# Cross attention's scores and outputs from operands split in rounded half and rest, in a two-block transformer kernel

## The reference

```python
def memory_cross_attention(h, m, wq, wk, wv, wo):      # h = rms_norm(x), m = rms_norm(mem)
    q = (h @ wq).reshape(B, S, CROSS_HEADS, CROSS_DH)  # 256 tokens, 4 heads of 256
    k = (m @ wk).reshape(B, M, CROSS_HEADS, CROSS_DH)
    v = (m @ wv).reshape(B, M, CROSS_HEADS, CROSS_DH)
    s = jnp.einsum('bshd,bmhd->bhsm', q, k).astype(jnp.float32) * (CROSS_DH ** -0.5)
    p = jax.nn.softmax(s, axis=-1).astype(h.dtype)
    o = jnp.einsum('bhsm,bmhd->bshd', p, v).reshape(B, S, D_MODEL)
    return o @ wo
```

## Time and profile before

| what | value |
| --- | --- |
| median of 3 runs | 2339.91 us (2339.79 to 2341.52) |
| the profiled execution | 2339.71 us, its span 2337.9 us |
| TensorE busy | 2327.7 us, 100% |
| VectorE busy | 1549.7 us, 66% |
| ScalarE busy | 1203.0 us, 51% |
| granted TensorE clock over the span | 0.999 |

### The profile page before, as it was taken

How to read it: one execution, slowest core, us unless ns; L and a number is a source line. 1 busy time by engine, 2 the same in 40 slices (tenths; PEclk the granted TensorE clock), 3 DMA queues, 4 the chain that set the end, 5 groups by cost and what they waited for, 6 DMA issues and landing times.

```text
span 2337.9 us, 33592 instructions
## 1 busy us (share of the span) xinstructions
PE 2327.7 (100%) x13127; PEld 2008.6 (86%) x13127; DVE 1549.7 (66%) x1427; ACT 1203.0 (51%) x1209; POOL 79.7 (3%) x47
## 2 busy tenths in 40 slices
PE   9999999999999999999999999999999999999999
PEld 8889888888888898888888888888888888888887
DVE  6667866666666687556667666476667667467666
ACT  5447665544544575545445445664445444565444
POOL 0000510000000033000000000000000000000000
PEclk9999999999999999999999999999999999999999
DMA  9555444555565563536556656546655556555653
GB/s 308 187 194 177 149 155 162 171 187 190 189 195 186 185 188 129 168 122 224 187 183 223 193 188 194 162 153 207 192 190 187 194 188 198 181 163 165 204 187 118
DMA packets 328903, 427.95 MB, mean 183 GB/s; under 512 B 15528, under 2 KB 294320, under 8 KB 328560
## 3 DMA queue, kind: packets, MB, share of 16 engines
q1 hardware_dynamic: 324832, 412.73, 55.0%
q10 hardware_dynamic: 3984, 13.97, 1.6%
HBM read 425.60 MB, written 1.05 MB: 182 GB/s over the span
## 4 chain that ended last, share of the span: by engine, by line
PE 96%; DVE 2%; ACT 1%; issue 1%; ACTq 0%; DVEq 0%
PE ps L1122 25%; PE ps L1008 17%; PE ps L1009 17%; PE ps L1010 17%; PE ps L1126 13%; PE ps L1021 1%; DVE wlo L1673 1%; PE ps L1482 1%; PE ps L1460 1%; ACT whi L511 1%; PE ps L1316 0%; DVE arena L2011 0%; PE ps L1384 0%; PE ps L1394 0%; PE ps L1532 0%
## 5 line engine op out<-in xcount | busy, mean ns | idle before, releaser
L1673 DVE TENSOR_TENSOR wlo<-raw,whi 128x2048 fp32r<-128x2048 f32 x390 | 897.8, 2303 | 513.1 <-ACT whi L511 512.9
L511 ACT ACTIVATE whi<-raw 128x2048 fp32r<-128x2048 f32 x392 | 746.3, 1905 | 559.0 <-PE ps L1010 330.7
L1122 PE MATMUL ps<-hT,whi 128*128 128x512 f32 x2560 | 610.7, 390 | 0.0
L1122 PEld LDWEIGHTS ps<-hT,whi 128*128 128x128 f32 x2560 | 474.9, 188 | 95.1
L1008 PE MATMUL ps<-whi,hT 128*128 128x512 f32 x920 | 369.1, 401 | 0.2
L1010 PE MATMUL ps<-whi,hT 128*128 128x512 f32 x920 | 359.3, 391 | 0.0
L1009 PE MATMUL ps<-wlo,hT 128*128 128x512 f32 x920 | 358.8, 390 | 0.0
L1126 PEld LDWEIGHTS ps<-hT,wlo 128*128 128x128 f32 x2560 | 329.3, 191 | 13.1
L1126 PE MATMUL ps<-hT,wlo 128*128 128x256 f32 x2560 | 333.3, 283 | 0.0
L1008 PE MATMUL ps<-whi,aT_hi 128*128 128x512 f32 x640 | 250.0, 391 | 0.0
L1009 PE MATMUL ps<-wlo,aT_hi 128*128 128x512 f32 x640 | 250.0, 391 | 0.0
(11 more groups left out here) (296 smaller groups left out, 1949.5 us busy)
## 6 DMA issues: line engine op xcount, KB each, us to landing
raw<-in_w_ffn SPq DMA_DIRECT2D x264, 512.0 KB, 4.3
raw<-in_w_in SPq DMA_DIRECT2D x144, 512.0 KB, 4.8
raw<-in_ffn_w_down SPq DMA_DIRECT2D x88, 512.0 KB, 4.2
raw<-in_ffn_w_up SPq DMA_DIRECT2D x86, 512.0 KB, 4.0
raw<-in_ffn_w_gate SPq DMA_DIRECT2D x86, 512.0 KB, 4.9
raw<-in_w_out SPq DMA_DIRECT2D x32, 512.0 KB, 4.1
gain<-in_gains ACTq DMA_DIRECT2D x16, 512.0 KB
raw<-in_cross_wk SPq DMA_DIRECT2D x16, 512.0 KB, 4.2
```

Of the source, the lines that this page charges most:

```text
L511: act.activation(whi[:, s, :, 0:cols], raw[:, s, :, 0:cols], ACT.Copy).then_inc(hi_ready, 1)
L1122: pe.matmul(ps[:, G + n, :], whi[:, s, k, n * P:(n + 1) * P], both[k], start=first and k == 0, stop=False, skip_group_check=True)
L1673: dve.tensor_tensor(wlo[:, s, :, 0:cols], raw[:, s, :, 0:cols], whi[:, s, :, 0:cols].bitcast(F32), ALU.subtract).then_inc(lo_ready, 1)
```

## The change

Every product of cross attention's scores and outputs becomes three products of rounded half and rest, and both parts are made for all four of its operands. The new tiles lie at the same addresses as the float32 ones of the arena, under the type float32r (`rounded`).

- `banks_out` writes the rounded half of keys and values and signals `kv_hi`; the new `rest_out(n)` on DVE waits for it, subtracts the half from the two PSUM banks, and signals that the banks are free. `TAKEN` now names V for these.
- `query_out(i)` on ACT copies the two banks of the unscaled queries as rounded half, `queries(i)` on DVE is now the subtraction. The inverse root and the 1/16 become a column of two numbers (`sst[:, 3, 8:10]`), which `cross_exp` takes as a per-partition scale beside its per-partition bias, and by which `cross_max` multiplies the maximum. `row` and `row_out` are gone here.
- `prob_lo(h)` on DVE subtracts the rounded probabilities from PSUM; `cross_turn(h + 1)` and `cross_out(h)` wait for it (`c_pT_lo`) instead of `cross_pT`.

```diff
-TAKEN = ("SVVVVSS" "SSSSVV", "SVSSSSSSSSS")
+TAKEN = ("SVVVVSS" "VVVVVV", "SVSSSSSSSSS")
...
             def banks_out(b, l, u, banks, dst):
...
-                last.then_inc(chunk_out, 1)
+                last.then_inc(kv_hi, 1)
...
-                row_out(row_no(0, l, 2))
+                def query_out(i):
+                    wait_unit(act, 0, l, A_Q + 2 * i + 1)
+                    for n, bank in enumerate(Q_BANKS[i]):
+                        act.activation(query_hi[i][:, n * 512:(n + 1) * 512], ps[:, bank, :], ACT.Copy).then_inc(c_query, 1)
+                query_out(0)
...
-                                              bias=sst[:, 1, i:i + 1], accum_out=sst[:, 2, i:i + 1])
+                                              scale=sst[:, 3, 8 + t:9 + t], bias=sst[:, 1, i:i + 1], accum_out=sst[:, 2, i:i + 1])
...
-                            mm = pe.matmul(ps[:, TR + h % 2, t * SEQ:(t + 1) * SEQ], q[:, at + t * P:at + (t + 1) * P], k_[:, at:at + SEQ],
-                                           start=(k == 0), stop=(k == 1))
+                            mm = split_product(ps[:, TR + h % 2, t * SEQ:(t + 1) * SEQ], query_hi[i][:, q], query_lo[i][:, q],
+                                               key_hi[i][:, keys], key_lo[i][:, keys], k == t == 0, k == 1)
...
-                            mm = pe.matmul(ps[:, HEAD_BANKS[h], j * SEQ:(j + 1) * SEQ], v[:, at:at + P], cp_t[h % 2][:, k * SEQ:(k + 1) * SEQ],
-                                           start=(k == 0), stop=(k == 1))
+                            mm = split_product(ps[:, HEAD_BANKS[h], j * SEQ:(j + 1) * SEQ], value_hi[i][:, v], value_lo[i][:, v],
+                                               cp_hi[h % 2][:, keys], cp_lo[h % 2][:, keys], j == k == 0, k == 1)
...
-                row(row_no(0, l, 2), norm_no(0, l, 3))
...
+                def rest_out(n, dst, hi, banks):
+                    dve.wait_ge(kv_hi, 4 * l + n + 1)
+                    for j, bank in enumerate(banks):
+                        at = slice(j * 512, (j + 1) * 512)
+                        last = dve.tensor_tensor(dst[:, at], ps[:, bank, :], hi[:, at].bitcast(F32), ALU.subtract)
+                    last.then_inc(feat_out, 1)
...
                 fox_max(2)
+                rest_out(0, key_lo[0], key_hi[0], KV_BANKS[0])
                 fox_max(3)
...
                 split_lo(0, l, A_OUT + 1)
+                rest_out(3, value_lo[1], value_hi[1], KV_BANKS[3])
...
+                step(dve.tensor_scalar(sst[:, 3, 8:10], stat[:, 0, 2, :], C_D ** -0.5, None, ALU.mult))
...
+                def prob_lo(h):
+                    dve.wait_ge(c_pT, l * C_HEADS + h + 1)
+                    if h >= 2:
+                        dve.wait_ge(turned, PIECES * T5 + h - 1)
+                    dve.tensor_tensor(cp_lo[h % 2], ps[:, G, :], cp_hi[h % 2].bitcast(F32), ALU.subtract).then_inc(c_pT_lo, 1)
...
                 split_lo(0, l, A_O + 1)
-                queries(1, fq)
+                prob_lo(0)
+                queries(1)
+                prob_lo(1)
                 head_lo(0)
...
                 cross_norm(3)
+                prob_lo(2)
                 split_lo(0, l, A_O + 2)
                 head_lo(2)
+                prob_lo(3)
                 split_lo(0, l, A_O + 3)
```

More of the change, by code:

```diff
@@ L40 @@
 S_A, S_B = 5, 2
-V_A, V_B = 28, (12, 10)
+V_A, V_B = 29, (12, 10)
 A_FFN1 = 0
@@ L66 @@
 FIRST_TURN = (0, DEPTH * 7)
-ROWS = (4, 3)
+ROWS = (3, 3)
 NORMS = (5, 3)
@@ L169, in build @@
         hst = sb("hst", [P, 3, 8])
+        with nc.sbuf_tensor("rounded", [P, 18432], F32R) as rounded:
+            pass
         arena = sb("arena", [P, 18432])
@@ L201, in build, with as_rounded @@
         MEM_BANKS = ((4, 5), (6, 7))
-        cp_t = (att[:, 0:512], att[:, 512:1024])
+        def as_rounded(*names):
+            at = {"zf": 2, "hq": 3, "hk": 4, "hv": 5, "hg": 6, "fq": 7, "fk": 8, "fv": 9, "cum": 10, "tmp1": 11, "tmp2": 12, "att": 15, "attx": 16, "fcs": 17}
+            return [rounded[:, at[n] * 1024:(at[n] + 1) * 1024] for n in names]
+        key_hi, key_lo = as_rounded("zf", "hq"), as_rounded("cum", "tmp1")
+        value_hi, value_lo = as_rounded("hk", "hv"), as_rounded("fk", "fv")
+        query_hi, query_lo = as_rounded("hg", "fq"), as_rounded("tmp2", "fcs")
+        cp_hi, cp_lo = ([m[:, h * 512:(h + 1) * 512] for h in range(2)] for m in as_rounded("att", "attx"))
         HEAD_BANKS = (0, 2, 5, 6)
@@ L282, in build @@
             sem(f"a_{n}") for n in ("score", "masked", "max", "prob", "norm", "turn", "pT", "out"))
-        c_score, c_max, c_prob, c_turn, c_pT = (sem(f"c_{n}") for n in ("score", "max", "prob", "turn", "pT"))
+        c_score, c_max, c_prob, c_turn, c_pT, c_pT_lo, c_query, c_scale, kv_hi = (
+            sem(f"c_{n}") for n in ("score", "max", "prob", "turn", "pT", "pT_lo", "query", "scale", "kv_hi"))
         r_rot, r_turn, r_kT, r_score, r_dec, r_out, r_sq, r_sum, r_rms, r_y, r_yT, r_hi, r_lo = (
@@ L814, in _ @@
                 fox_exp(1)
-                banks_out(0, l, A_K, KV_BANKS[0], zf)
+                banks_out(0, l, A_K, KV_BANKS[0], key_hi[0])
                 fox_pT(0)
@@ L825, in _ @@
                 fox_exp(5)
-                banks_out(0, l, A_K + 2, KV_BANKS[1], hq)
+                banks_out(0, l, A_K + 2, KV_BANKS[1], key_hi[1])
                 fox_pT(4)
@@ L834, in _ @@
                 split_hi(0, l, A_V + 3)
-                banks_out(0, l, A_V, KV_BANKS[2], hk)
+                banks_out(0, l, A_V, KV_BANKS[2], value_hi[0])
                 split_hi(0, l, A_OUT)
@@ L840, in _ @@
                 split_hi(0, l, A_OUT + 1)
-                banks_out(0, l, A_V + 2, KV_BANKS[3], hv)
+                banks_out(0, l, A_V + 2, KV_BANKS[3], value_hi[1])
                 for i in (0, 1):
@@ L875, in cross_pT @@
                         act.wait_ge(turned, PIECES * T5 + h - 1)
-                    act.activation(cp_t[h % 2], ps[:, G, :], ACT.Copy).then_inc(c_pT, 1)
+                    act.activation(cp_hi[h % 2], ps[:, G, :], ACT.Copy).then_inc(c_pT, 1)
                 def head_hi(h):
@@ L2102, in _ @@
                 fox_norm(5)
+                rest_out(1, key_lo[1], key_hi[1], KV_BANKS[1])
                 fox_max(6)
@@ L2107, in _ @@
                 split_lo(0, l, A_V + 2)
+                rest_out(2, value_lo[0], value_hi[0], KV_BANKS[2])
                 split_lo(0, l, A_V + 3)
@@ L2126, in _, with queries @@
                 inverse(norm_no(0, l, 3))
+                step(dve.tensor_scalar(sst[:, 3, 8:10], stat[:, 0, 2, :], C_D ** -0.5, None, ALU.mult))
                 split_lo(0, l, A_Q + 3)
                 T5 = turn_no(0, l, 5)
[L2130 to L2133 removed]
+                def queries(i):
                     for n, bank in enumerate(Q_BANKS[i]):
[L2135 to L2137 removed]
+                        at = slice(n * 512, (n + 1) * 512)
+                        dve.wait_ge(c_query, 4 * l + 2 * i + n + 1)
+                        last = dve.tensor_tensor(query_lo[i][:, at], ps[:, bank, :], query_hi[i][:, at].bitcast(F32), ALU.subtract)
                     last.then_inc(feat_out, 1)
```

16 lines of the change are left out of this document (10 added, 6 removed).

## The result

The changed kernel takes 2348.49 us, median of 7 runs (2348.14 to 2349.03); the kernel before took 2340.22, measured beside it (7 runs, 2339.79 to 2342.77). The ratio is 1.0032, 95% interval 1.0023 to 1.0042: slower by 0.3%, 8.3 us, where 2346.7 was predicted. The profiled execution took 2348.51, its span 2346.5, 8.6 more than the span before.

What follows compares the result with a forecast made beforehand. TensorE was taken as the bound, busy 2327.7 of 2337.9 us. Per layer, bank waits 1.3 + 1.3 and cross attention 1.0 make 3.6, twice 7.2: 2346.9 (2345.4 at the lower operand price); 2346.7 was taken, range 2343 to 2349.5.

Steps and rivals of the forecast that it cites:

- The two bank waits: TensorE waits for DVE's subtractions at `free(7)` (second half of `A_K + 2`) and `free(10)` (`A_OUT`), 1.3 us each per layer.
- `free(8)`, `free(9)` and the split of `A_V + 3`: Hand-overs of keys and values claimed to cost nothing; the split comes 2.8 us later with 2.5 to spare.
- The three waits of cross attention: TensorE waits at `cross_turn(1)` 1.2, at `A_O` for `head_lo(1)` 1.3, at `cross_out(2)` 1.05 us per layer.
- The second operand: Exponential's added per-partition scale: between 0 and 96 ns, 0.096 us taken; 2346.9 at the dearer price, 2345.4 at the lower.
- The products are cheaper: Head products: twelve split products in 1.44 us for 1.72 in float32; with the row gone, 4.9 us saved in all.
- cross attention, 1.0 a layer: Cross attention becomes 1.0 us longer per layer: 3.5 of waits against 2.4 saved and a little at the hand-over.
- the sum of 2346.9: Whole kernel: 3.6 us per layer, twice 7.2, added to 2339.7; 0.3% slower.
- no cheaper: Rival: 256-column products from the new tiles slower, 0.14 us each would take the whole saving; 2349; 5 in 100.
- stalls dearer: Rival: clock or restart makes each of ten stalls dearer, 0.3 us more each; 2350; 8 in 100.
- Only the saving counts: Rival: all waits are hidden, leaving 2339.7 - 4.9 = 2334.8; 4 in 100.
- the chain of `head_lo(1)`: Cross attention: DVE ends `head_lo(1)` at 407.4, PE wants it for `A_O` from 406.1: wait 1.3 us.
- the bank rival: Rival: bank waits hidden or half as long, 2340.1 to 2344.3; decides at a DVE step below 0.35 us; 12 in 100.

Runs made afterwards that it cites:

- e1: Changed kernel with the first keys' rest (`rest_out(0)`) moved ahead of head 2's maximum on DVE: 2346.03 us, ratio 1.0025.
- e2: Changed kernel with the last values in PSUM banks 4 and 5, and TensorE's wait for them moved ahead of the queries: 2346.52 us, ratio 1.0028.
- e6: Changed kernel with e1, e2 and e5 in one, and the rest of values 2 and 3 behind the attention part's halves: 2336.70 us, ratio 0.9984.
- e5: Changed kernel with cross attention's lists on ACT, DVE and TensorE in another order, same instructions: 2341.81 us, ratio 1.0006.
- e7: Changed kernel with the edit of e5 on TensorE alone: 2345.56 us, ratio 1.0021.
- e8: Changed kernel with the edits of e5 on ACT and DVE alone: 2344.91 us, ratio 1.0021.
- e3: Changed kernel with the exponential's scale a constant instead of a per-partition operand, the queries' inverse root left out of the scores: 2346.65 us, ratio 1.0028.
- e9: Kernel before the change, float32 head products kept, with e5's order of cross attention's lists: 2339.71 us, ratio 0.9999.
- e4: Changed kernel without rests of keys, values and probabilities, halves in their place, same three passes, `rest_out` and `prob_lo` gone: 2338.97 us, ratio 0.9994.

## Why the prediction was right, and by how much it missed

**The two bank waits: right, in place, cause and size.** Each was put at 1.3 a layer. By the starts of the products behind them they add 1.62 - 0.32 = 1.30 and 2.96 - 1.62 = 1.34. e1 and e2 took them away one by one; e6 shows that neither is needed. `free(8)`, `free(9)` and the split of `A_V + 3` cost nothing, as argued: no row of the waits names them.

**The three waits of cross attention: right in place and order, one too short.** The prediction counted its waits from start to start. So counted they are 1.47, 1.34 and 1.05 for 1.2, 1.3 and 1.05 (idle times 1.31, 1.18 and 0.89). The chain was followed correctly: e5, e7 and e8 broke it at the links that it names.

**The second operand: the dearer of the two prices.** 0.559 was measured for the 0.567 taken, and the difference to 0.470 in e3 is 89 ns. The prediction gave the difference between the prices 1.5 us of the whole time; e3 measured 1.5.

**The products are cheaper, by the rows' sum.** Twelve in 1.42 for 1.44 predicted. The rival by which they would not be is out: e6 stands 3.6 below before with stalls of 1.4 left, together 5.0, against 4.9 predicted, and e9 says that cross attention's lists did not bring it.

**The mis-sized term: cross attention, 1.0 a layer, measured at 1.5.** The prediction's own clock starts the scores at 389.6. Timeline of PE and DVE in the changed kernel, start of the first score and the step that `cross_turn(1)` waits for:

```profile
392.60 0.28 PE L1027 MATMUL ps<-rounded 128*128 128x256 f32 x1
...
402.29 0.68 DVE L2198 TENSOR_TENSOR rounded<-ps,rounded 128x512 fp32r<-128x512 f32 x1
```

So all before it adds 3.0. With that the prediction's points become 402.9 for `cross_turn(1)`, 410.4 for `A_O`, 414.6 for `cross_out(2)` and 422.1 for the end of `cross_out(3)`; the trace has 403.12, 410.68, 415.04 and 422.57. The excess is 0.2, 0.3, 0.4 and 0.5. At `cross_turn(1)` the stall is 0.27 longer than the 1.2: 0.15 of it is between DVE's end at 402.97 and PE's transposition at 403.12, where nothing had been allowed and the other four waits show 0.05; the rest is DVE 0.07 later and TensorE 0.05 earlier than worked out. Then 0.11 is the first product of `A_O`, 411.02 - 410.68 = 0.34 where one in a row takes 0.23, and 0.10 the first of `cross_out(2)`, 415.26 - 415.04 = 0.22 for 0.12. With the 0.04 by which the wait at `A_O` is longer that makes the 0.5.

The two dear first products look like the price of starting again after a wait, but they are not. Second product of `A_O` in the kernel before, where the first came at 406.79 and no wait is listed, and the first two of `cross_out(2)` in e4, without a wait:

```profile
407.12 0.39 PE L1009 MATMUL ps<-wlo,hT 128*128 128x512 f32 x1
```

```profile
410.32 0.37 PE L1027 MATMUL ps<-rounded 128*128 128x256 f32 x1
410.53 0.28 PE L1028 MATMUL ps<-rounded 128*128 128x256 f32 x1
```

They took 0.33 and 0.21 there. So the prediction missed a tenth at the first product of each of these two pieces, because it priced every product as one in a row, waiting or not.

Per layer 2.68 (3.0 less 0.32) for the banks, where 2.6 was predicted, and 1.47 for cross attention, where 1.0 was, twice 8.3, and 0.3 for the late start give the span's 8.6.

**Of the rivals** two are nearer to the measured 2348.5 than the sum of 2346.9: "no cheaper" with 2349 and "stalls dearer" with 2350. By the time alone they would not be out; the rows put them out. Twelve products take 1.42, and a first product behind a wait takes within 0.01 of what it takes without one (0.34 and 0.33, 0.22 and 0.21), with no change of clock (the granted clock is 1.0 over the span of the changed kernel too). "Only the saving counts" was refuted by the first row of waits, and e4 adds that even without any of the new DVE steps most of the saving would have been lost at `A_O`. That the chain of `head_lo(1)` would hold the saved products back by itself was in the working (before, `A_O` started "with hardly any" wait) but was not said as a conclusion.

**What stays open.** e6 comes 0.5 lower than the sum of e1, e2 and e5 and of the 0.8 at L2150 that e2 had left, which is within what these runs can tell. Why the transposition at `cross_turn(1)` starts 0.15 behind DVE's end, and not 0.05, was not followed up. No run changed the DVE step's own length, so the point at which the bank rival would decide (0.35 us) is only argued.

## What to carry to other kernels

When one engine is busy all the time, an operand's new preparation step costs nothing on the average and everything at the place where it is due: list for each operand when the bound engine wants it and when the chain gives it, before counting the products saved. A buffer that is now handed back by a second engine comes free at that engine's place in its list; move that step ahead, or put the data in a buffer that is wanted later, and look what stood behind it. A change that makes the bound engine faster and its feeders later should be judged with its lists re-ordered: here the same arithmetic is 0.32% slower in the old order and 0.16% faster in the new.

## What the runs showed that was not expected

- The second per-partition operand of an activation costs as much as the first: 470 (e3) and 559 ns, 89 more, beside 96 for the first one, also in a form that accumulates. The Trainium skill, page "ScalarE: Activation LUTs", section "What ACT_TABLE_LOAD costs", puts each at some 93 ns; these traces agree.
- TensorE loses more at a wait than the idle time in its row: 0.16 more in this kernel, at 256 as at 512 columns, since a product's record ends that much after the next start is due. At ten waits it comes to 1.7 us, and only with it does the sum of saving and waits (8.3) come near the span's 8.6; with the idle times alone it is 6.6.
- Waits at different places of a list are nearly additive: taking away the first, the second and the last three one at a time gave 2.1, 1.7 and 6.8 us, all at once 11.9, which includes the 0.8 of waiting that the second had uncovered.
